# Attention's rows times their inverse norm, in the convolution stage: GpSimd in the place of VectorE

## The reference, cut to what matters

```python
def _rmsnorm(x, g):
    x32 = x.astype(F32)
    return x32 * lax.rsqrt(jnp.mean(x32 * x32, axis=-1, keepdims=True) + NORM_EPS) * g.astype(F32)
...
    o_da = _diff_attention(qh, keys, vals, lam)
    o_da = _rmsnorm(o_da, p['diff_subln_g']) * (1.0 - lam_init)
    o_hy = _hyena_mixer(hy, filt_f, p['hy_skip'], p['hy_conv_w'], p['hy_conv_b'])
    mix = jnp.concatenate([o_hg, o_da, o_hy], axis=-1) @ p['w_out'].astype(F32)
```

## Time and profile before

| | before |
|---|---|
| median of 3 runs | 4248.17 us (4247.88 to 4252.54) |
| profiled execution, its time | 4250.18 us |
| profiled execution, its span | 4248.3 us |
| granted TensorE clock, mean | 0.961 |
| VectorE busy | 1655.6 us (39%) |
| ScalarE busy | 1091.9 us (26%) |
| GpSimd busy | 168.0 us (4%), 102 instructions |

### The profile page before, as it was taken

The page is one execution under the profiler, slowest core; times in us unless marked ns, Lnnn a source line. Parts: engine busy times, 40 slices in busy tenths (PEclk is TensorE's granted clock), DMA queues, the critical chain, the costliest instruction groups (busy, mean ns, idle before and its releaser), DMA issues. The chain is left out here.

```text
span 4248.3 us, 56917 instructions
## 1 busy us (share of the span) xinstructions
PE 3930.1 (93%) x24230; PEld 3113.9 (73%) x24230; DVE 1655.6 (39%) x2974; ACT 1091.9 (26%) x2662; POOL 168.0 (4%) x102
## 2 busy tenths in 40 slices
PE   7999999989968999999899999989899599999996
PEld 3566875667437999999745779656664299999995
DVE  4247723878442111111141487248783511111111
ACT  3351212871110111111133422138601111111112
POOL 0000001000000000000000000110000000000000
PEclk9999999999978999999999999999999799999998
DMA  8311022011345788877482110210122468877874
GB/s 295 142 36 59 29 78 76 1 52 57 126 166 182 270 282 283 283 268 263 166 313 101 41 48 29 85 67 1 61 85 105 164 218 283 277 263 271 283 269 179
DMA packets 323595, 664.55 MB, mean 156 GB/s; under 512 B 22470, under 2 KB 60998, under 8 KB 320784
## 3 DMA queue, kind: packets, MB, share of 16 engines
q1 hardware_dynamic: 311536, 617.92, 40.2%
q0 software_dynamic: 9216, 33.56, 3.4%
q10 hardware_dynamic: 2592, 9.44, 0.5%
HBM read 594.80 MB, written 66.08 MB: 156 GB/s over the span
## 5 line engine op out<-in xcount | busy, mean ns | idle before, releaser
L2103 PE MATMUL ps<-arena 128*128 128x144 f32 x8192 | 1015.4, 287 | 10.3 <-DVE arena L2263 10.3
L2103 PEld LDWEIGHTS ps<-arena 128*128 128x128 f32 x8192 | 1008.5, 190 | 17.9 <-DVE arena L2263 17.9
L291 PE MATMUL ps<-arena 128*128 128x384 f32 x1920 | 628.6, 488 | 10.2 <-PEq L89 10.2
L291 PEld LDWEIGHTS ps<-arena 128*128 128x128 f32 x1920 | 364.1, 191 | 259.2 <-issue 14.8
L2127 PE MATMUL ps<-arena 128*128 128x144 f32 x4096 | 507.1, 286 | 0.0
L2127 PEld LDWEIGHTS ps<-arena 128*128 128x128 f32 x4096 | 503.6, 190 | 0.0
L2274 DVE TENSOR_TENSOR arena<-arena,ps 128x144 f32<-128x144 f32 x256 | 77.9, 304 | 920.6 <-ACT arena L2179 920.6
L2179 ACT ACTIVATE arena<-ps 128x144 f32<-128x144 f32 x256 | 74.5, 291 | 1012.2 <-PE ps L2103 1012.2
L433 ACT ACTIVATE arena<-ps 128x384 f32<-128x384 f32 (+1 forms) x192 | 86.2, 449 | 691.7 <-PE ps L291 460.8
L288 PE MATMUL ps<-arena 128*128 128x256 f32 x1152 | 257.0, 381 | 0.0
L2263 DVE TENSOR_SCALAR arena<-ps,mod 128x128 f32<-128x128 f32 x256 | 87.0, 403 | 435.5 <-PE ps L2083 435.5
(11 more groups left out here) (315 smaller groups left out, 3692.4 us busy)
## 6 DMA issues: line engine op xcount, KB each, us to landing
arena<-in_w_gate SPq DMA_DIRECT2D x64, 2048.0 KB, 8.1
arena<-in_w_up SPq DMA_DIRECT2D x64, 2048.0 KB, 14.0
arena<-in_w_down SPq DMA_DIRECT2D x64, 2048.0 KB, 12.3
arena<-in_w_mod SPq DMA_DIRECT2D x24, 2048.0 KB, 11.9
arena<-in_w_in SPq DMA_DIRECT2D x28, 1024.0 KB, 5.2
arena<-in_dft_units SPq DMA_DIRECT2D x48, 512.0 KB, 6.5
arena<-x_rows SPq DMA_DIRECT2D x29, 512.0 KB, 4.6
arena<-in_x SPq DMA_DIRECT2D x18, 512.0 KB, 4.3
```

Source lines behind the costliest of these rows:

```text
L291: last = nc.tensor.matmul(m.ps[:, at:at + TC], m.Wr[:, slot % 2, k, jj * P:(jj + 1) * P], m.hT[:, k, q * TC:(q + 1) * TC], start=(k == 0), ...
L2103: last = nc.tensor.matmul(m.ps[:, at:at + CAP], m.wbuf[:, 2 * h + which, k, q * P:(q + 1) * P], m.xe[:, e % 2, k, :], start=(k == 0), stop ...
```

## The change

The product of `o_att` with its inverse norms is issued by GpSimd, in an instruction stream of its own for this stage, and no longer by VectorE. GpSimd waits for a new semaphore, `rows_scale`, which VectorE's reciprocal raises; the wait of VectorE for its own reciprocal is gone. `rows_ready`, for which TensorE waits, is raised by GpSimd. Operands, shape and place of the result are the same.

```diff
@@ -1492,7 +1492,7 @@
-               "tap", "tapped", "turned_in", "hu_ready", "hu_ctx", "forward", "product", "spectra", "inverse", "result",
+               "tap", "tapped", "rows_scale", "turned_in", "hu_ready", "hu_ctx", "forward", "product", "spectra", "inverse", "result",
@@ -1542,6 +1542,12 @@
+        @block.gpsimd
+        def _(pool):
+            pool.wait_ge(s["rows_scale"], 1)
+            nc.gpsimd.tensor_tensor(o4, o4, sm.unsqueeze(3).to_broadcast([P, NT, HEADS, DV]), ALU.mult)\
+                .then_inc(s["rows_ready"], 1)
@@ -1841,9 +1847,7 @@
                 dve.wait_ge(s["root"], 1)
-                c.then_wait(dve, nc.vector.reciprocal(m.small[:, 0:n_rows], m.small[:, 0:n_rows]))
-                nc.vector.tensor_tensor(o4, o4, sm.unsqueeze(3).to_broadcast([P, NT, HEADS, DV]), ALU.mult)\
-                    .then_inc(s["rows_ready"], 1)
+                nc.vector.reciprocal(m.small[:, 0:n_rows], m.small[:, 0:n_rows]).then_inc(s["rows_scale"], 1)
```

## The result

The changed kernel takes 4256.59 us (median of 20 runs, 4251.68 to 4261.05) against 4249.70 us before (20 runs, 4247.60 to 4254.13): 6.9 us more, a ratio of 1.0016 with a 95% interval of 1.0009 to 1.0023. That is 3.8 to 9.8 us slower. The sign and the mechanism are those forecast; the size is a little over half of the 12.2 us.

What follows compares the result with a forecast made beforehand. VectorE's chain was taken to set the end before ctx_forward(0). Per layer, 5.0 us of later products plus 1.1 of clock make 6.1, 12.2 for two: 4260.4 us from a median of 4248.17, range 4252 to 4267.

Steps and rivals of the forecast that it cites:

- What bounds the stage: Before ctx_forward(0), VectorE's chain sets the end; TensorE idles 4.92 us there, so a microsecond on VectorE is one of TensorE.
- GpSimd's product doesn't run beside `short`: Behind the reciprocal, GpSimd blocks VectorE in the middle of short; products start 5.0 us later per layer; chance 0.66.
- The size of GpSimd's product: At the moved 128x4608 product: GpSimd takes 9.9 us, kept between 8.7 and 11.3, with 15.2 as far end.
- The clock: At ctx_forward(0), the granted clock falls inside the longer idle time and TensorE restarts low: +1.1 us per layer, bounds 0 and 1.1.
- Cover and queues: At TensorE's turns (L1566), rows are ready 0.5 us before being asked for, at no cost; DMAs behind att_turned go out as before.
- A: At short: GpSimd and VectorE run side by side at unchanged lengths; -6.6 us per layer, 4235.0 us; chance 0.10.
- B: At short: VectorE goes first, GpSimd enters at the first products, first sum waits 8.6 us; +3.7 per layer, 4255.6; chance 0.10.
- C: From short through the products: GpSimd yields to VectorE's two-input operations, TensorE waits at L1566; +4.4 per layer, 4257.0; chance 0.08.
- D: At the moved product: a slow GpSimd takes 15.2 us; 11.4 us more per layer with clock, 4271 us; chance 0.06.

Runs made afterwards that it cites:

- both together: The changed kernel (product on GpSimd) with ScalarE's square of attention's output also moved ahead of take_in(0); 4245.72 us, ratio to the kernel before 0.9990.
- four of nine tiles: Changed kernel with six PSUM products ahead of short(2) and short(3), GpSimd taking only four tiles of the product, VectorE five; 4244.72 us against 4249.35 before.

## Why the prediction was right, and where its sizes were off

*What bounds the stage.* Right. Product left out and squares moved ahead are two unlike ways to shorten VectorE's chain by 4.9 and 4.4 us; both take TensorE's wait at `ctx_forward(0)` to 0.4 us or less, and give 12.8 and 13.0 us.

*GpSimd's product doesn't run beside `short`.* Right, and in the place named: the first filter operation gets in ahead, GpSimd begins behind it, and the next operation of L1833 stands for the whole of the product. The one-input reduction (3.70 us) and the six PSUM products (3.68 us) pass, the sums and filters don't. The Trainium skill's rule (SBUF — State Buffer, "SBUF: two separate sides") is that the pair of ports is locked for a whole instruction, against VectorE operations with two SBUF inputs. The 7.98 us for 127 elements agree. That the one that starts first holds the pair agrees too, in both directions: VectorE's 7.98 us here, and GpSimd's 6.25 us for 3.5 us of work behind VectorE's product.

*The size of GpSimd's product.* This is the term that was mis-sized. I took 9.9 us from a row with two full inputs and never asked whether this product's second input is a full one; it is one norm for each 128 values. The full one measures 9.95, this one 7.89. The estimate was right for another operation, and the true value lay below my lower bound of 8.7. Even for that other one it was partly luck: GpSimd alone takes 2.34 us for 1024 elements, not the 2.19 that I read from the earlier trace rows, and 4.5 x 2.34 would be 10.5. The 1.26 us of the earlier trace rows are not a product's either: L1085 adds, also with two full inputs.

VectorE stood 7.98 - 0.34 = 7.6 us, not 9.9, in exchange for the 4.87 that it gave up, and the products came 2.55 us later per layer, not 5.0: 4.9 us of the 5.3 by which the forecast was too high. Of the 2.45 per layer 2.0 are the product's length (9.9 - 7.9). Most of the other 0.4 lies in how I put the pieces end to end: the first filter operation starts 0.30 us behind the reciprocal's start, not 0.38, and GpSimd's 7.89 us hold VectorE for only 7.64.

*The clock.* It fell inside the idle time, as said; in the stretches of 1 us of the changed kernel (columns as in the earlier trace rows):

```profile
1007.00:1008.00 1.00, 0.00 (x0) 0.63 0.00 0
1009.00:1010.00 1.00, 0.33 (x1) 0.50 0.00 0
1014.00:1015.00 1.00, 1.00 (x4) 0.95 0.00 0
```

It is back 4.4 us after the restart at 1009.67 (5.1 in the second layer), not 5.7; a loss of 2.2 to 2.5 us instead of the 1.7 before the change. The term is +0.5 to +0.8 per layer, not +1.1: inside its bounds, and the second size that was off. With the products' 2.55 this is 3.1 to 3.3 per layer; the trace has 3.0 and 3.3.

*Cover and queues.* Right: the rows were ready at 965.90 and TensorE asked at 968.6, with no wait for GpSimd anywhere; the DMAs behind `att_turned` went out after the twelfth group as before.

*The rivals.* A fell with L1833 at 7.98 us; its price was right (4235.0, and 4236.4 without the product). B and C fell by the trace, and only by it: they stood at +7.4 and +8.8 us, both nearer to the measured +6.9 than the forecast's +12.2, and +6.9 lies below the forecast's own lower bound of +7.6. That the time lies in the range says little for the mechanism, and the kernel before, at 4249.70 us instead of the 4248.17 that I started from, helped it there by 1.5. What decides is that a waiting GpSimd gets in between two adjacent operations of VectorE, in the changed kernel after the first and in the nine pieces after every one. D fell: of the 3.38 us in the earlier trace rows only 2.34 are GpSimd's own length at 1024 elements; the other 1.0 was waiting. The chance of 0.68 for slower by over 0.2% was given to a size that the change doesn't have: 0.16%, with an interval from 0.09 to 0.23%, counts as "same" by that bound, to which I gave 0.22.

## What to carry to other kernels

Before a product goes from VectorE to GpSimd, list what VectorE does next. Here filter operations and sums with two SBUF inputs stood until the GpSimd instruction was done (7.98 us for 0.34), while a reduction with one SBUF input and products with one input from PSUM ran on at their length. Size the GpSimd part to that cover (this gave 4.6 us); cutting it in nine pieces shortened each stand to some 0.7 us but gained nothing over the kernel before (one run). Take the duration from an operation with the same kind of second input: full or broadcast. And look first at why the chain that sets the end starts when it does: here one line of ScalarE's order gave 13.0 us, where the move to GpSimd cost 6.9.

## What the runs showed of the hardware that I had not expected

A GpSimd product with one input broadcast over 128 values takes 1.71 ns an element (7886 / 4608), one with two full inputs 2.16 (9948 / 4608); at 1024 elements it is 1895 against 2344 ns. The GPSIMD Engine Reference of the Trainium skill (3.1 "Elementwise — side-by-side cycle accounting") gives 2.6 cycles an element for two inputs, which at its 1.2 GHz is an estimate of 10.0 us for 4608 elements. The full product (9.95 us) agrees, the broadcast one (7.89) doesn't, and the measurement decides.

In one execution of one kernel (both together, the two rows above), a wait of 3.36 us in front of `ctx_forward(0)` left the granted clock at full in layer one, and a shorter one of 2.85 us found it at half on resuming in layer two: L1634 takes 2.07 us instead of 1.13. With four of nine tiles it was 2.50 us with half on resuming in layer one, and 2.83 with the clock full in layer two. So the length of the wait alone doesn't tell whether the clock falls; what does was not tested.
